# Six column groups instead of five in the channel-quarter rounds, x tiles placed later, and another layout of the attention biases

## The reference

```python
mods = silu(c) @ w_ada + b_ada                 # shift1, scale1, gate1, shift2, scale2, gate2
h = rmsnorm(x, g_pre1) * (1 + scale1) + shift1
q, k, v, f, u, bg, cg, ga, gb = split(h @ w_in)
logf = log_sigmoid(f + b_f); cum = cumsum(logf)
# attention, 16 heads of 64; samples also see 256 cached rows in 2 pages
p = softmax(q @ k.T / 8 + cum[q] - cum[k], causal);  o = p @ v
# convolution part
y = bg * conv3_causal(cg * u)
m = (sigmoid(ga) * (o @ w_oa) + sigmoid(gb) * (y @ w_ob)) @ w_o
x = x + gate1 * rmsnorm(m, g_post1)
x = x + gate2 * rmsnorm(swiglu(rmsnorm(x, g_pre2) * (1 + scale2) + shift2), g_post2)
```

## Time and profile before

| | us |
|---|---|
| median of 3 runs | 1828.35 (1828.08 to 1828.42) |
| the profiled execution, its own time | 1830.57 |
| span of its trace | 1828.9 |
| PE busy | 1802.0 |
| DVE busy | 881.1 |
| ACT busy | 708.2 |

### The profile page before, as it was taken

One profiled execution on the slowest core, in us unless ns is written; L12 is line 12 of the kernel. 1 busy time (PEld: TensorE's weight loads), 2 busy tenths in 40 slices (PEclk: granted clock), 3 DMA queues, 4 the chain that ended last, 5 costly groups with the idle time before them and its releaser, 6 DMA issues.

```text
span 1828.9 us, 32073 instructions
## 1 busy us (share of the span) xinstructions
PE 1802.0 (99%) x13775; PEld 1683.2 (92%) x13775; DVE 881.1 (48%) x1065; ACT 708.2 (39%) x829; POOL 25.5 (1%) x77
## 2 busy tenths in 40 slices
PE   8999999999999999999999999999999999999997
PEld 6788988897599999998969999999999999999996
DVE  3556753234644343453465334344443445566565
ACT  4333223334643333343364323333333334545453
POOL 0001000010000000000000000000000000000000
PEclk9999999999999999999999999999999999999999
DMA  9997879865564445549837464444444444444541
GB/s 321 361 358 264 298 292 332 305 251 190 210 228 162 163 167 166 171 165 348 320 134 256 166 225 169 169 165 161 161 161 165 168 166 167 162 161 162 163 159 53
DMA packets 193881, 382.40 MB, mean 209 GB/s; under 512 B 8981, under 2 KB 17645, under 8 KB 193487
## 3 DMA queue, kind: packets, MB, share of 16 engines
q1 hardware_dynamic: 190032, 378.04, 59.2%
q0 software_dynamic: 1328, 2.58, 0.4%
q10 hardware_dynamic: 2424, 0.37, 0.2%
HBM read 376.15 MB, written 4.81 MB: 208 GB/s over the span
## 4 chain that ended last, share of the span: by engine, by line
PE 94%; DVE 2%; DMA 1%; ACT 1%; issue 1%; SPq 0%; DVEq 0%; ACTq 0%
PE bank L615 29%; PE bank L617 28%; PE bank L616 28%; PE bank L625 4%; PE bank L853 1%; DMA x_rows<-in_x_sample 1%; PE bank L987 1%; DMA ada<-in_w_ada 1%; PE bank L634 1%; PE bank L672 0%; PE bank L956 0%; DVE xT L2163 0%; PE bank L906 0%; PE bank L923 0%; PE bank L832 0%
## 5 line engine op out<-in xcount | busy, mean ns | idle before, releaser
L615 PE MATMUL bank<-a_lo,w_hi 128*128 128x288 f32 x3648 | 1085.7, 298 | 6.7 <-DVE a_lo L1750 3.3
L616 PE MATMUL bank<-a_hi,w_hi 128*128 128x288 f32 x3648 | 1076.9, 295 | 0.0
L617 PE MATMUL bank<-a_hi,w_lo 128*128 128x288 f32 x3648 | 1073.1, 294 | 0.0
L1609 DVE TENSOR_TENSOR w_lo<-raw,w_hi 128x2048 fp32r<-128x2048 f32 x240 | 550.1, 2292 | 709.5 <-ACT w_hi L1156 708.9
L1156 ACT CAST w_hi<-raw 128x2048 fp32r<-128x2048 f32 x239 | 456.0, 1908 | 867.2 <-PE bank L617 819.8
L615 PEld LDWEIGHTS bank<-a_lo,w_hi 128*128 128x128 f32 x3648 | 684.2, 188 | 25.7 <-issue 19.4
L617 PEld LDWEIGHTS bank<-a_hi,w_lo 128*128 128x128 f32 x3648 | 687.6, 188 | 0.0
L616 PEld LDWEIGHTS bank<-a_hi,w_hi 128*128 128x128 f32 x3648 | 685.6, 188 | 0.0
L1709 DVE TENSOR_TENSOR a_lo<-hid,a_hi 128x1152 fp32r<-128x1152 f32 x44 | 59.4, 1352 | 12.3 <-ACT a_hi L1186 12.3
L625 PE MATMUL bank<-ada,cT 128*32 128x512 f32 (+1 forms) x608 | 63.0, 551 | 0.5 <-DMA ada<-in_w_ada 0.5
L1186 ACT CAST a_hi<-hid 128x1152 fp32r<-128x1152 f32 x44 | 50.8, 1156 | 0.0
(11 more groups left out here) (293 smaller groups left out, 949.1 us busy)
## 6 DMA issues: line engine op xcount, KB each, us to landing
raw<-in_w_ffn_in SPq DMA_DIRECT2D x88, 1024.0 KB, 4.9
raw<-in_w_in SPq DMA_DIRECT2D x76, 1024.0 KB, 9.0
ada<-in_w_ada SPq DMA_DIRECT2D x60, 1024.0 KB, 9.5
raw<-in_w_ffn_out SPq DMA_DIRECT2D x44, 1024.0 KB, 5.1
ada_o<-in_w_ada SPq DMA_DIRECT2D x26, 1024.0 KB, 9.6
raw<-in_w_o SPq DMA_DIRECT2D x16, 1024.0 KB, 5.5
ada<-in_w_ada SPq DMA_DIRECT2D x16, 512.0 KB, 9.7
raw<-in_cache_k SPq DMA_DIRECT2D x16, 512.0 KB, 4.6
```

What stands on the lines that cost most here:

```text
L615: pe.matmul(acc, w_hi[buf][:, a, cols], lo[:, kt, :], start=first and a == 0, stop=False)
L616: pe.matmul(acc, w_hi[buf][:, a, cols], hi[:, kt, :], start=False, stop=False)
L617: mm = pe.matmul(acc, w_lo[buf][:, a, cols], hi[:, kt, :], start=False, stop=last and a == tiles - 1)
L1609: tt(w_lo[buf][:, :, :], raw[s][:, :, :], w_hi[buf][:, :, :].bitcast(F32), ALU.subtract).then_inc(raw_turn, 1)
```

## The change

`CUT` becomes 6: B's second half is a sixth column group of the rounds, summed in a new tile `acc_B1`. There are 28 rounds; the four products of `N_B1` and ACT's copies into `yT` are gone. SP's loads, PE's groups and the work of ACT and DVE are written in a new order around them; the convolution of the first half now stands between the last rounds on DVE. At the start x tiles 10 to 15 are turned later, behind and among the slots of the second modulation visit. In attention the picking matmul uses rounded operands (a high and a low part of `ncum` in rows 0 to 15 and 64 to 79, and `pick`) over 80 rows; the samples' bias is no longer added by PE but lies in a tile `bias_s` of all partitions and is added by DVE together with the maximum (`max_sample`); ACT's exponential reads SBUF, not PSUM. PE's waits for `sS_exp` become waits for `sS_max`.

```diff
-    CUT = 5
+    CUT = 6
     ROUNDS = EARLY + CUT * (KT // SK)
...
-        round_cols = (CU, CC, CB, CU + SN, CC + SN)
+        round_cols = (CU, CC, CB, CU + SN, CC + SN, CB + SN)
...
             load_first(3)
-            load_rounds(4, 8)
+            load_rounds(4, 10)
             load_first(4)
-            load_rounds(8, 10)
+            load_rounds(10, 11)
             load_first(5)
-            load_rounds(10, 11)
+            load_rounds(11, 12)
             load_first(6)
-            load_rounds(11, 14)
+            load_rounds(12, 14)
             load_first(7)
-            load_rounds(14, 16)
+            load_rounds(14, 18)
             load_first(8)
-            load_rounds(16, 19)
+            load_rounds(18, 20)
             load_first(9)
-            load_rounds(19, ROUNDS)
...
+            load_rounds(20, 24)
+            for q in range(SK):
+                load_ada(SK * A_B1 + q, q, wv_ada[q, :, :, (A_B1 - SPARE) * SN:(A_B1 - SPARE + 1) * SN])
+            load_rounds(24, ROUNDS)
...
-            for n in range(EARLY, 2 * EARLY):
+            for n in range(EARLY, 2 * EARLY + 1):
                 round_product(n)
             ada_group(4)
-            round_product(2 * EARLY, 4)
+            round_product(2 * EARLY + 1, 4)
             ada_group(5)
...
                 round_product(n + 2, v)
                 round_product(n + 3)
                 ada_group(v + 1)
...
-                round_product(n + 4, None, shift_transposes)
-            for n in range(EARLY + 3 * CUT, ROUNDS):
+                round_product(n + 4, v + 1)
+                round_product(n + 5)
+            n = EARLY + 3 * CUT
+            round_product(n)
+            round_product(n + 1)
+            ada_group(A_B1)
+            round_product(n + 2, A_B1)
+            for n in range(EARLY + 3 * CUT + 3, ROUNDS):
                 round_product(n)
...
-                    pick = ident[r0:r0 + H, r0 + 2 * s + j:r0 + 2 * s + j + 1].broadcast_to([H, P])
-                    pe.matmul(bank[j][:, 0:3 * P], pick, ncum[r0:r0 + H, :], start=True, stop=False,
-                              tile_position=(r0, 0), skip_group_check=True)
+                    h = 2 * s + j
+                    pe.matmul(bank[j][:, 0:3 * P], pick[:, h:h + 1].broadcast_to([DH + H, P]), ncum[:, :],
+                              start=True, stop=False, skip_group_check=True)
...
-                for c in range(CT):
-                    pe.matmul(bank[6][32 * c:32 * c + 32, 0:KEYS], selq[:, c, :], cumk[:, s, :], start=True, stop=False,
-                              tile_position=(0, 32 * c))
...
             later_round(n + 1)
             split_round(n + 3)
             make_z(0, u_t, acc_C, n + 1)
+            add_ada(A_B1, A_B1)
             later_round(n + 2)
             split_round(n + 4)
+            conv_tile(0, 0)
+            conv_tile(0, 1)
             later_round(n + 3)
             split_round(n + 5)
+            conv_tile(0, 2)
+            conv_tile(0, 3)
             later_round(n + 4)
             make_z(1, acc_u1, acc_C1, n + 4)
...
             def copy_sums():
                 dve.wait_ge(suf_ps, 1)
...
+                n = SB * NPG * H // 2
+                for j in range(2):
+                    rows = suf[j][:, :, :, 0, :].rearrange("p s c (q t) -> p (s c) q t", t=ST)
+                    src = bank[7][:, n * j:n * j + n].rearrange("p (s q) -> p s q", q=4)
+                    ins = nc.vector.tensor_copy(rows, src.unsqueeze(3).broadcast_to([P, n // 4, 4, ST]))
+                ins.then_inc(suf_done, 1)
                 dve.wait_ge(cum_ps, 1)
-                for p0 in (0, DH):
-                    own.mark(ts(ncum[p0:p0 + H, 0:P], bank[6][p0:p0 + H, 0:P], -1.0, None, ALU.mult))
-                    own.mark(ts(ncum[p0:p0 + H, P:3 * P], bank[6][p0:p0 + H, 0:TP], -1.0, None, ALU.mult))
...
+                own.mark(nc.vector.memset(ncum[:, :].bitcast(F32), 0.0))
+                own.mark(nc.vector.tensor_copy(pick[:, :], ident[0:DH + H, 0:H]))
+                own.wait()
+                own.mark(nc.vector.tensor_copy(pick[DH:DH + H, :], ident[DH:DH + H, DH:DH + H]))
+                for c0, c1 in ((0, 0), (P, 0), (TP, P)):
+                    own.mark(ts(ncum[0:H, c0:c0 + P], bank[6][0:H, c1:c1 + P], -1.0, None, ALU.mult))
+                own.wait()
+                for c0, c1 in ((0, 0), (P, 0), (TP, P)):
+                    own.mark(stt(ncum[DH:DH + H, c0:c0 + P], bank[6][0:H, c1:c1 + P], -1.0,
+                                 ncum[0:H, c0:c0 + P].bitcast(F32), ALU.mult, ALU.subtract))
                 for s in range(SB):
...
+                    own.mark(nc.vector.tensor_copy(bias_s[:, s, at_], bank[7][:, at_]))
...
-                own.mark(nc.vector.tensor_reduce(small[:, 8:9], bank[6][:, 0:KEYS], AX.X, ALU.max))
+                if s > 0:
+                    dve.wait_ge(sP_ps, s)
+                else:
+                    dve.wait_ge(sufT_done, 1)
+                own.mark(nc.vector.tensor_tensor_reduce(
+                    s_s[:, :], bank[6][:, 0:KEYS], bias_s[:, s, :], 1.0, MASKED, ALU.add, ALU.max, small[:, 8:9]))
```

More of the change, by code:

```diff
@@ L695, in _ @@
             keep_warm(4)
[L696 to L702, removed]
+            for kt in range(X_DVE):
                 turn_x(kt)
             turn_rows_in()
[L705 to L706 removed]
+            for q in range(SK):
+                early_slot(q, 0)
             pe.wait_ge(diag_done, 1)
@@ L714, in _ @@
             ada_transpose(0, HALF)
+            for kt in range(X_DVE, X_DVE + 4):
+                turn_x(kt)
             pe.wait_ge(ada_copied, 2)
@@ L717, in _ @@
                 early_slot(q, 1)
+            for kt in range(X_DVE + 4, KT):
+                turn_x(kt)
             keep_warm(1)
@@ L770, in ada_beside @@
                     ada_transpose(g)
-            for t in range(SK):
-                product(N_B1 + t, t == 0, t == 3, G_B1, SK * t, a_hi, a_lo, t % SPLIT)
-                ada_beside(A_B1, t, ada)
             pe.wait_ge(s_wf, 16)
@@ L1238, in _, with copy_x @@
             first_root()
-            for kt in range(X_DVE, KT):
+            def copy_x(kt):
                 act.wait_ge(x_ps, kt + 1)
@@ L1243, in _ @@
             split_round(0)
+            for kt in range(X_DVE, X_DVE + 4):
+                copy_x(kt)
             copy_ada(1, SN // 2)
+            for kt in range(X_DVE + 4, KT):
+                copy_x(kt)
             split_h(0, 0)
@@ L1367, in exp_sample @@
                 act.wait_ge(sS_max, s + 1)
-                if s > 0:
-                    act.wait_ge(sP_ps, s)
-                nc.scalar.activation(s_s[:, :], bank[6][:, 0:KEYS], ACT.Exp, bias=small[:, 8:9],
+                nc.scalar.activation(s_s[:, :], s_s[:, :], ACT.Exp, bias=small[:, 8:9],
                                      accum_out=small[:, 9:10]).then_inc(sS_exp, 1)
@@ L2319, in _ @@
             pool.wait_ge(ada_turn, RAW + SK * ADA_MAIN)
+            own.mark(g.memset(bias_s[:, :, PAST:KEYS], MASKED))
+            own.mark(g.memset(newk[:, :], 0.0))
+            pool.wait_ge(s_zout, 32)
+            for j in range(2):
+                own.mark(g.memset(suf[j][:, :, :, 1, :], 0.0))
+            own.wait()
+            g.tensor_copy(newk[32:32 + ST, :].rearrange("u (s t) -> u s t", s=SB),
+                          c4[:, :].unsqueeze(1).broadcast_to([ST, SB, ST])).then_inc(fixed, 1)
+            pool.wait_ge(fixed, 1)
             own.mark(g.memset(upto[:, :], 1.0))
@@ L2327, in _ @@
             own.mark(g.memset(q_bd[:, :, :], 0.0))
-            own.mark(g.memset(cumk[:, :, :], 0.0))
             own.wait()
-            own.mark(g.memset(cumk[0:H, :, PAST:KEYS], MASKED))
-            for s in range(SB):
-                own.mark(g.tensor_copy(cumk[32:32 + ST, s, PAST + ST * s:PAST + ST * s + ST], c4[:, :]))
-            own.wait()
-            pool.sem_inc(fixed, 1)
             def samples_q(s):
```

121 lines of the change are left out of this document (53 added, 68 removed).

## The result

| | before | changed |
|---|---|---|
| median of 6 runs | 1829.28 us (1828.08 to 1837.24) | 1837.42 us (1836.17 to 1838.86) |
| ratio, 95% interval | | 1.0042 (1.0032 to 1.0051) |
| the profiled execution | 1830.57 us, span 1828.9 | 1837.11 us, span 1835.2 |

The account below looks back on a forecast made before the run. PE was taken as the bound, busy 1802.0 of 1828.9 us. New waits and start and bias costs against -6.5 for attention summed to +4.4 (1832.8 us); half-clock stretches added 2.6, giving 1835.4, range 1829.5 to 1840.

Follow-up runs that it names:

- e3: Changed kernel with the loads of rounds 14 and 20 queued ahead of their modulation groups, not behind: 1830.61 us, ratio 1.0005 to the kernel before.
- e6: Changed kernel with group 4 again ahead of round 8 and rounds 8 and 9 between groups 4 and 5: 1834.26 us, ratio 1.0028.
- e4: Changed kernel with one convolution tile in each of four places instead of two in each of two: 1835.8 us, ratio 1.0042.
- e5: Changed kernel with idle products of ones (5, 3 and 4) in the waits ahead of rounds 14, 20 and 26: 1834.44 us, ratio 1.0028.
- e9: Changed kernel with rounds 14 and 20's loads ahead of groups, single convolution tiles, group 4 ahead of round 8, every picking matmul issued twice: 1829.15 us.

## What to carry to other kernels

Where one engine is busy for 99%, a change that "moves" work is priced by the first consumer behind each moved transfer: take the start of the preceding group as zero and follow the slot through the queue, cast, split and the evicting add, as one would a timetable. A load that is needed first belongs ahead of the bulk loads whose buffers come free later, as soon as its own buffer is free; e3 won some 6.8 us with that alone. And on the vector engine a piece of work put between an eviction and the product that needs its bank must fit in the slack of one product: one tile of 1.86 us did, two did not.

## What was unexpected of the hardware

- The half clock behind a wait of 2 to 2.6 us comes in some executions and not in others: present behind 2.51 and 2.00 in the changed kernel and 1.91 in e6, absent behind 2.58 in e4 and 2.35 in e3, under the same order of work around them. Idle products in the waits saved 2.6 us by the ratios (e5), with the waits as long as before.
- A short group of rounded matmuls costs more than its columns: 0.175 us each for 384 columns, and 0.19 us once, of which 0.11 stands behind the first matmul and 0.09 ahead of the next line (e9).
- The time between the issue of a group of 4 MB and the release of PE by its last slot was 13.2 us in one order and 14.6 us in the other, while as many bytes as the group has landed within 12.4 and 12.5 us: a load can be complete well after its share of the bytes is in.
